# Three gate and up pieces moved between the first modulation units of a hybrid diffusion step

## What is computed

```python
mod = silu(c) @ w_ada + b_ada            # 9 x 2048 values for each of two conditions
h = rmsnorm(x, g[0]) * (1 + mod[1]) + mod[0]
x = x + 0.5 * mod[2] * rmsnorm((silu(h @ wg0) * (h @ wu0)) @ wd0, g[1])   # first feed-forward, D_FF = 5632
x = x + mod[5] * rmsnorm(mixer(...), g[3])                               # mLSTM and SSD heads
x = x + 0.5 * mod[8] * rmsnorm((silu(h @ wg1) * (h @ wu1)) @ wd1, g[5])   # second feed-forward
```

## Time and profile before

| | us |
|---|---|
| median of 3 runs | 3206.73 (3204.51 to 3207.51) |
| the profiled execution's own time | 3204.82 |
| its span | 3202.9 |
| TensorE busy | 3078.1 (96%) |
| GpSimd busy | 1837.7 (57%) |
| VectorE busy | 1366.0 (43%) |
| ScalarE busy | 983.1 (31%) |
| HBM read | 517.02 MB |

### The profile page before, as it was taken

One profiled execution on the slowest core, in us unless ns is written; L12 is line 12 of the kernel. 1 busy time (PEld: TensorE's weight loads), 2 busy tenths in 40 slices (PEclk: granted clock), 3 DMA queues, 4 the chain that ended last, 5 costly groups with the idle time before them and its releaser, 6 DMA issues.

```text
span 3202.9 us, 50063 instructions
## 1 busy us (share of the span) xinstructions
PE 3078.1 (96%) x18189; PEld 2957.6 (92%) x18189; DVE 1366.0 (43%) x3074; ACT 983.1 (31%) x1227; POOL 1837.7 (57%) x911
## 2 busy tenths in 40 slices
PE   6799999999999999799999999799999999999996
PEld 2499999999999999699999999699999999999996
DVE  0336665566556665585753353413343111110015
ACT  2232222222222223434432233432222222223222
POOL 2366556655566555446865445566555665666663
PEclk7799999999999999899999999899999999999998
DMA  9967666665656565345444545145554544434441
GB/s 335 296 209 225 196 196 196 223 199 190 210 196 225 196 196 177 124 133 161 139 135 119 124 110 165 60 127 183 170 177 138 164 125 126 129 124 125 127 127 40
DMA packets 537316, 530.13 MB, mean 166 GB/s; under 512 B 25115, under 2 KB 534531, under 8 KB 536579
## 3 DMA queue, kind: packets, MB, share of 16 engines
q1 hardware_dynamic: 505376, 507.57, 50.2%
q10 hardware_dynamic: 31843, 21.25, 2.4%
HBM read 517.02 MB, written 9.64 MB: 164 GB/s over the span
## 4 chain that ended last, share of the span: by engine, by line
POOL 39%; issue 28%; PE 26%; DVE 4%; DMA 2%; ACT 2%; POOLq 1%; ACTq 0%; DVEq 0%
POOL w_lo L2157 36%; PE banks L671 7%; PE banks L673 7%; PE banks L672 7%; POOL hid_lo L2177 1%; PE banks L731 1%; DMA AM<-in_w_in_dram 1%; DMA w_raw<-in_w_ada_dram 1%; DVE HB L1875 1%; PE banks L697 1%; DVE banks L1500 0%; PE banks L955 0%; PE banks L1040 0%; PE banks L1060 0%; ACT AM L1155 0%
## 5 line engine op out<-in xcount | busy, mean ns | idle before, releaser
L2157 POOL TENSOR_TENSOR w_lo<-w_raw,w_hi 128x1024 fp32r<-128x1024 f32 x668 | 1597.9, 2398 | 1096.9 <-ACT w_hi L1136 1096.7
L671 PE MATMUL banks<-xn_hi,w_hi 128*128 128x384 f32 x3936 | 1342.7, 341 | 29.2 <-DVE xn_lo L1517 18.4
L673 PE MATMUL banks<-xn_hi,w_lo 128*128 128x384 f32 x3936 | 1321.7, 336 | 0.0
L672 PE MATMUL banks<-xn_lo,w_hi 128*128 128x384 f32 x3936 | 1321.5, 336 | 0.0
L1136 ACT ACTIVATE w_hi<-w_raw 128x1024 fp32r<-128x1024 f32 x668 | 705.5, 1059 | 1521.1 <-PE banks L673 907.1
L671 PEld LDWEIGHTS banks<-xn_hi,w_hi 128*128 128x128 f32 x3936 | 743.9, 189 | 51.2 <-issue 37.1
L672 PEld LDWEIGHTS banks<-xn_lo,w_hi 128*128 128x128 f32 x3936 | 743.9, 189 | 3.6 <-issue 2.9
L673 PEld LDWEIGHTS banks<-xn_hi,w_lo 128*128 128x128 f32 x3936 | 743.3, 189 | 0.0
L1586 DVE SCALAR_TENSOR_TENSOR banks<-w_raw,cT,banks 128x256 f32<-128x256 f32 x1372 | 550.6, 481 | 0.3
L671 PE MATMUL banks<-hid_hi,w_hi 128*128 128x384 f32 x1408 | 474.0, 337 | 6.6 <-POOL hid_lo L2177 6.6
L673 PE MATMUL banks<-hid_hi,w_lo 128*128 128x384 f32 x1408 | 471.1, 335 | 0.0
(11 more groups left out here) (235 smaller groups left out, 1353.2 us busy)
## 6 DMA issues: line engine op xcount, KB each, us to landing
w_raw<-in_w_ada_dram SPq DMA_DIRECT2D x288, 512.0 KB, 5.1
w_raw<-in_ffn_w_gate_dram SPq DMA_DIRECT2D x176, 512.0 KB, 3.8
w_raw<-in_ffn_w_up_dram SPq DMA_DIRECT2D x176, 512.0 KB, 3.7
w_raw<-in_ffn_w_down_dram SPq DMA_DIRECT2D x176, 512.0 KB, 3.6
w_raw<-in_w_in_dram SPq DMA_DIRECT2D x104, 512.0 KB, 3.7
w_raw<-in_w_out_dram SPq DMA_DIRECT2D x32, 512.0 KB, 3.6
HB<-row_wait ACTq DMA_DIRECT2D x12, 512.0 KB, 5.0
x_wait<-xT ACTq DMA_DIRECT2D x1, 3072.0 KB, 9.6
```

What stands on the lines that cost most here:

```text
L671: pe.matmul(out, wh, hi, start=start, stop=False)
L672: pe.matmul(out, wh, lo, start=False, stop=False)
L673: return pe.matmul(out, w_lo[:, w, off:off + P], hi, start=False, stop=stop)
L2157: pool.tensor_tensor(w_lo[:, slot(p), :], w_raw[:, p % NR, :], w_hi[:, slot(p), :].bitcast(F32), ALU.subtract).then_inc(w_lo_ready, 1)
```

## The change

`LEAD_BODY` loses six "m": the pieces g and u of q = 0, 1 and 2 move into `START_PIECES`, behind units 8, 10 and 13. The loads keep this new order; positions in it are 0 to 69 for the prologue (g and u at 36 and 37, 46 and 47, 60 and 61), 76 and 81 for g and u of q = 3, and from 91 on for the other eight main pieces. The loads of x are issued after 4 pieces instead of 8. x is transposed one tile after every piece from position 6 on. Pairs 0 to 6 stand at v = 6, 7, 8, 9, 10, 12, 14. On ScalarE and GpSimd the splits of the moved pieces stand at v = 7, 9 and 12; the splits of positions 76, 81 and 91 stand before the feed-forward, on GpSimd now behind the clearing of `y`. In the first part, for its first 256 columns, ScalarE splits ahead after the Silu instead of before. Where one "a" unit follows another without a main piece, its columns are asked for after piece q = 1 of the next.

```diff
-PAIR_AT = 9
-LEAD_BODY = 2 * "aaam" + 6 * "aam" + 2 * SPREAD_END
+LEAD_BODY = "aaaaaamaaaamaaaaaaaa" + 2 * SPREAD_END
...
-        main = [(kind, 0, q) for q in range(U) for kind in "gu"] + main[-2 * U:]
+        main = [(kind, 0, q) for q in range(0 if n else U - 1, U) for kind in "gu"] + main[-2 * U:]
...
-START_PIECES = ada_units(ADA_FIRST)
+START_MAIN = {8: 0, 10: 1, 13: 2}
+START_PIECES = []
+for v in range(ADA_FIRST):
+    START_PIECES += [("a", v, q) for q in range(U)]
+    if v in START_MAIN:
+        START_PIECES += [(kind, 0, START_MAIN[v]) for kind in "gu"]
+START_AT = {piece: p for p, piece in enumerate(START_PIECES)}
+START_PAIRS = {6: 0, 7: 1, 8: 2, 9: 3, 10: 4, 12: 5, 14: 6}
+N_START = len(START_PIECES) - U * ADA_FIRST
...
# first_tile
-    g = U * v + q - late - U - 1
-    return g // 2 if g >= 0 and g % 2 == 0 and g // 2 < KT else None
+    t = U * v + q - late - U - 2
+    return t if 0 <= t < KT else None
...
# SyncE
-                for v, unit in enumerate(ADA_START):
-                    if v == 2:
+                for p, (kind, v, q) in enumerate(START_PIECES):
+                    if (kind, v, q) == ("a", 1, 0):
...
# TensorE, prologue
-                        ada_piece(U * v + q, q, v)
+                        ada_piece(START_AT["a", v, q], q, v)
+                        if first_tile(v, q, 3) == KT - 1:
+                            added_sum("x0")
...
+                    if v in START_MAIN:
+                        for b, kind in enumerate("gu"):
+                            unit_piece(START_AT[kind, 0, START_MAIN[v]], START_MAIN[v], 2 * b, fresh=0)
...
# TensorE, feed-forward
                                 ada_piece(p, q, ada_unit(n, part, s), i, per)
+                                if q == 1 and pending is not None:
+                                    ada_columns(pending, i)
+                                    pending = None
...
# ScalarE, feed-forward
-                            if kind not in "ab":
+                            early = part == "first" and n == 0 and s == 0
+                            if kind not in "ab" and not early:
                                 split(p, i, per)
                             if kind in "gu" and q == U - 1:
                                 posts(it0, s, kind, p, i, per)
+                            if kind not in "ab" and early:
+                                split(p, i, per)
...
# ScalarE, prologue
-                    if v > PAIR_AT:
-                        first_tiles(v - 1 - PAIR_AT)
-                first_tiles(KT // 2 - 2)
-                for p in MAIN[:AHEAD - 1]:
+                    if v in START_PAIRS:
+                        first_tiles(START_PAIRS[v])
+                    if v + 1 in START_MAIN:
+                        for kind in "gu":
+                            make_hi(START_AT[kind, 0, START_MAIN[v + 1]])
+                first_tiles(KT // 2 - 1)
+                for p in MAIN[N_START:N_START + AHEAD]:
                     make_hi(p)
-                first_tiles(KT // 2 - 1)
-                make_hi(MAIN[AHEAD - 1])
                 ffn(0)
...
# VectorE, feed-forward
                             if kind == "a":
+                                if q == 1 and pending is not None:
+                                    ada_store(pending, i)
+                                    pending = None
...
# VectorE, prologue
+                    if v == min(START_PAIRS):
+                        dve.wait_ge(xT_ready, KT)
+                        inverse_root("x0")
                     if v:
                         ada_store(v - 1, t0=2 * ADA_START[v - 1])
...
-                    if v >= PAIR_AT:
-                        first_tiles(v - PAIR_AT)
-                    ada_rows_out(U * v + U - 1, v)
+                    if v in START_PAIRS:
+                        first_tiles(START_PAIRS[v])
+                    ada_rows_out(START_AT["a", v, U - 1], v)
...
# GpSimd
-                even_low(0, range(0, KT - 2, 2))
-                for p in MAIN[:AHEAD - 1]:
-                    make_lo(p)
-                even_low(0, range(KT - 2, KT, 2))
-                make_lo(MAIN[AHEAD - 1])
+                for v in range(ADA_FIRST):
+                    if v in START_PAIRS:
+                        even_low(0, (2 * START_PAIRS[v],))
+                    if v + 1 in START_MAIN:
+                        for kind in "gu":
+                            make_lo(START_AT[kind, 0, START_MAIN[v + 1]])
+                even_low(0, (KT - 2,))

                 pool.wait_ge(xt_tr, KT)
                 pool.memset(y[:, :, :], 0.0).then_inc(y_zeroed, 1)
+                for p in MAIN[N_START:N_START + AHEAD]:
+                    make_lo(p)
                 ffn(0)
```

More of the change, by code:

```diff
@@ L630, in ffn @@
                         load(tail_of(n) + j, w_down[n][:, D_FF // P - PK:, PC * j:PC * j + PC])
-                for v, unit in enumerate(ADA_START):
-                    if v == 2:
+                for p, (kind, v, q) in enumerate(START_PIECES):
+                    if (kind, v, q) == ("a", 1, 0):
                         sp.dma_start(x_tok[:, 0, :], A["x_prompt"][0]).then_inc(x_loaded, 16)
                         sp.dma_start(x_tok[:, 1:3, :], A["x_sample"][0].rearrange("(c p) n -> p c n", p=P)).then_inc(x_loaded, 16)
-                    for q in range(U):
-                        load(U * v + q, block_of(w_ada, unit * PC, q))
+                    load(p, block_of(w_ada, ADA_START[v] * PC, q) if kind == "a" else block_of(w_gate[0] if kind == "g" else w_up[0], 0, q))
                 ffn(0)
@@ L767, in _ @@
                             vectors((0, 1, 2, 3))
-                        if first_tile(v, q, 4) == KT - 1:
-                            added_sum("x0")
                         t = first_tile(v, q)
@@ L1696, in _ @@
                         dve.wait_ge(vec_ready, 2)
-                    if v == PAIR_AT:
-                        dve.wait_ge(xT_ready, KT)
-                        inverse_root("x0")
-                    if v >= PAIR_AT:
-                        first_tiles(v - PAIR_AT)
-                    ada_rows_out(U * v + U - 1, v)
+                    if v in START_PAIRS:
+                        first_tiles(START_PAIRS[v])
+                    ada_rows_out(START_AT["a", v, U - 1], v)
                 ada_store(ADA_FIRST - 1, t0=2 * ADA_START[-1])
```

## The result

The changed kernel takes 3215.78 us, the median of 7 runs (3213.34 to 3218.56), against 3206.73 of 7 runs of the kernel before (3202.49 to 3207.51): a ratio of 1.0031 [1.0021, 1.0041]. It is 9.05 us slower; 3215.2 was predicted. The execution that was profiled is the slowest of the seven, 3218.56 us with a span of 3216.6.

The account below looks back on a forecast made before the run. Bound: TensorE, 96% busy, though the prologue is bound by full DMA engines. A chain of seven steps moved the first part's end from 210.1 to 218.6 us: 3206.7 + 8.5 = 3215.2 us, range 3200 to 3225.

Parts of the forecast that it names:

- The end of the first part is what counts: TensorE's end of the last up piece: any delay or gain before 210 us is carried to the end one for one.
- the chain: Successive estimated times from the sooner x to the first part's last up piece: end 218.6 against 210.1 before, +8.5 us.
- Step 1: Prologue, x issued sooner: TensorE's sixth tile still starts at 44.8, reciprocal at 64.2 us instead of 79.8.
- Step 2: First moved pair, position 36: high part 77.7, low part 80.1, g to 86.3, u to 90.5 us.
- Step 3: Second moved pair, position 46, reusing the slot of 38 after a 4.4 us refill: ready 98.9, pair ends 108.0 us.
- Step 4: Third moved pair, position 60, landing behind 56 to 59: ready 122.4, pair ends 132.3 us.
- Step 5: GpSimd clears y, 5.2 us, ahead of position 76's low part: g of q = 3 from 151.9 to 158.9 us.
- Step 6: ScalarE's Silu waits behind position 91's high part (172.8): row copy 177.2 us, TensorE's columns stalled 8 to 10 us.
- Step 7: From the stalled columns to the first part's end, TensorE cold at first: position 91 4.9 us, end 218.6 against 210.1.
- The queue of loads is the only bound: Rival, chance 0.12: the ring doesn't run dry, position 91 lands at 154.5, first part ends 200.3, -9.8 us, 3197.
- No change: Rival, chance 0.28: refills at the low end (-3) and a clock that mostly stays up (-5): +0.5 us, 3207.
- Much slower: Rival, chance 0.08: gate weights late and every g cold, +16.5 us, 3223.

Follow-up runs that it names:

- The dummies: The changed kernel with unused matmuls added in TensorE's stall ahead of the columns of unit 18: nine 3216.54 us, fifteen 3213.19 us.
- Silu and clear together: The changed kernel with position 91's high part behind the first Silu and y cleared right behind the squares of x: 3208.02 us, 1.0007.
- the reorder with its three repairs: The changed kernel with moved pieces placed one by one, position 91's high part behind the first Silu, and y cleared early: 3200.3 us, 0.9985.

## Why the prediction was right

**The end of the first part is what counts.** Held: +9.05 us in the medians. What lies behind the end is 1.7 us longer, which is within the 4.8 us that it scatters over all these kernels (2990.0 to 2994.8 us). But in the profiled executions the part ended 11.9 us later rather than 8.5, so the chain came out 3.4 us short. That the median lies within 0.6 us of the forecast is in part luck: the sum carries the before's execution, 1.9 us under its median, while the execution of after is 2.8 us over its own.

**Step 1, x sooner.** Reciprocal 60.64 for 64.2. Mis-sized: I had held GpSimd's pad clear at 38.30, since the small gate weights seemed to come when they came. They landed at 34.39. They are issued on ScalarE's queue at the same time as before (10.84 for 11.01), while x is issued 5.6 us sooner on SyncE's; with x sooner they landed sooner, and TensorE's sixth tile came sooner with them (40.91 for 44.8). The bound of 3 us that I had put on it was nearly the size.

**Step 2, first g and u.** The 3.6 us were lost again at once, because position 36 was bound by its load: high part 75.36 for 76.6, matmuls 78.90 for 80.1, u's end 89.6 for 90.5.

**Step 3.** 97.73 for 98.9, end 107.6 for 108.0. The refill went nearly as priced: issue 90.26, matmuls 7.5 us later, where 4.4 + 1.06 + 2.4 is 7.9.

**Step 4.** 122.94 for 122.4, end 133.8 for 132.3: this g was colder, 10.8 us for the pair where I had 9.9.

**Step 5, the clear.** Low part 146.7 for 144.3, the clear right behind it, g of q = 3 at 154.22 for 151.9. Shown by the experiment that moves it, with 3.6 us back in the trace. Here my reading was short of two things. VectorE's row copy waits for the clear too, and TensorE's columns behind it take 4.08 of the 4.9 us that TensorE idles there; I had named only the low part. And in the kernel before the same clear cost no less (3199.0 without it, 6.3 us). It belongs in the sum of after, as it stood, but not on the bill of the change.

**Step 6, the Silu behind a load.** High part of 91 at 174.86 for 172.8, row copy's end 179.2 for 177.2, a stall of 10.05 us where 8 to 10 were named. Removing it gave 6.65 us of the end. The seven loads up to 91 went as priced: the first was issued at 161.30, the high part began 13.56 us later, where 4.4 + 6 x 1.5 is 13.4.

**Step 7.** 6.4 us from the columns to position 91 as forecast, then that piece took 6.1 for 4.9, still cold. End 222.16 for 218.6. The cold pieces are the second term that was too small: the five gate pieces of steps 2 to 5 and 7 took 31.4 us where I had 28.7 (a pair less 4.17 for its u, and the two single ones). The dummies show 1.7 us for the last of them. By the same prices my upper bound was too low: 24 matmuls of 0.32 us are 7.7 us, and four gate pieces that are cold throughout would add 7.0 us, not 5.

**The rivals.** "The queue of loads is the only bound" (3197) failed by the run-dry ring: DMA share 0.70, 0.71 and 0.53 around the pairs. Feeding the pieces singly took back 6.5 us of the end and the whole loss in the medians, though Silu and clear stand in that kernel as they stood. I had the ring in the chain only as four refills; it is a cause of its own. Whether it is larger than the Silu is open: the ends give 6.5 us for the ring, 6.65 for the Silu and 3.6 for the clear, the medians, each against the kernel before that ran beside it, 8.1, 4.9 and 3.0. Whether the three add up is open too: together they give 18.7 us by the ends, where the sum is 16.8, and 14.1 by the medians, where it is 15.9. "No change" (3207) wanted short refills and a clock that stays up; neither came: the refills took 4.0 us for position 46 and 4.6 in step 6, and each of the five gate pieces began cold, at 0.32 us a matmul. "Much slower" (3223) wanted the gate weights late; they came 3.9 us sooner.

**Refills.** From the issue of position 46's load (90.26) to its matmuls (97.73) it is 7.47 us. Less the high part and the low part, 3.46, that leaves 4.0 for the load, between the two rows that I had priced it by; ScalarE was busy until it took this piece up, so the load may have been in sooner. The Trainium skill, "DMA: Bandwidth & Descriptors", section "Anatomy of one DMA", gives the fixed 2.0 us plus bytes at 436 GB/s for transfers that GpSimd issues; these loads are issued by SyncE, which the prediction did not say. By it the load would take 3.2 us, as an estimate. The trace speaks for the rows: the seven loads of step 6, for which ScalarE stood waiting, bear the 4.4 us out.

What stays open: how much of the 9 us each cold gate piece cost, since the clock was tested behind the last stall only; and why the medians of Silu and clear together lie 2.7 us above the kernel before, when the end in the trace is 0.5 later.

## What to carry to other kernels

Work that is moved into a stretch where an engine idles isn't free if that stretch is bound by loads in a ring: while the moved piece holds TensorE, no slot comes free, and what the queue misses comes back later as a stall. Move it in single pieces, and look at the DMA share over each. Before a reorder, look at what stands in the queue of each engine ahead of an instruction that many wait for (a clear, the high part of a late load ahead of a Silu): here moving one clear by itself (3199.0) was worth as much as the reorder with its three repairs (3200.3).

## What was not expected of the hardware

A small transfer, the gate weights, landed 3.9 us sooner (38.30 to 34.39) when the large one of x was issued 5.6 us sooner on another engine's queue, while its own issue hardly moved. It held in every kernel here: 34.2 to 34.9 in the twelve with x sooner, 38.3 and 38.9 in the two without.

Filling a part of a stall gave nothing: with 6.07 us of matmuls and 4.26 us idle behind them the columns took 1.01 us, the same as behind 10.05 us of nothing, and with 9.94 us of matmuls and no gap 0.61.
